# Two transformer blocks in float32r halves: four weight units side by side behind a sandwich norm, a reordered preamble, wide stick-breaking blocks first, and the last square of a row norm summed by TensorE

## The chip, the cores and the metric

The kernel runs as one program on one core of a Trainium2 chip. The metric is the time of one execution in microseconds (us) on the device, as the median of the runs; lower is better.

## The reference

Two blocks of two layers each work on x, 512 tokens by 1024 channels, in float32. Cut to what matters here:

```python
# first block, for each of two layers
h = rms_norm(x, attn_pre_g[l]); proj = h @ w_in[l]            # 1024 x 3080: q, k, v of 4 difference heads and
                                                              # 8 forgetting heads, and 8 forget logits
oa = rms_norm(diff_attention(rotary(qa), rotary(ka), va, lam), diff_sub_g[l]) * (1 - lam_init)
ob = forgetting_attention(qb, kb, vb, log_sigmoid(f_logit + forget_bias[l]))
x = x + rms_norm(concat(oa, ob) @ w_out[l], attn_post_g[l])   # sandwich norm: before and behind
h = rms_norm(x, ffn_pre_g[l])
y = (silu(h @ w_gate[l]) * (h @ w_up[l])) @ w_down[l]         # 2816 wide
x = x + rms_norm(y, ffn_post_g[l])
# second block: stick-breaking attention (layer 0), HGRN2 (layer 1), each with a squared-relu MLP (4096)
q, k, v = split(rmsnorm(x, g) @ w_qkv)                        # 16 heads of 64; q and k normed per head
z = q @ k.T * scale                                           # per block of 128 queries, causal
log_between = reverse_cumsum(log_sigmoid(-z)) - log_sigmoid(-z)
weights = exp(log_sigmoid(z) + log_between)                   # strictly causal
x = x + (weights @ v) @ w_o
```

## The kernel before

Everything is kept transposed: `xT` holds x as 8 tiles of 128 channels by 512 tokens. Each weight matrix is used in units, one unit being 128 output channels. A unit's weights (128 x 1024, 512 KB) are loaded by a DMA on SP's queue into `w_raw[:, slot]` (slot 0 or 1, in turn), rounded by GpSimd to float32r as `w_hi` (L571) and subtracted by VectorE to the rest `w_lo` (`split_low`, L1181). The activations are likewise halves, `h_hi` from ScalarE (L1679) and `h_lo` from VectorE (`low_part`, L1111), and TensorE runs for each of 8 input tiles hi x hi, hi x lo and lo x hi (`products`, L618): 24 products of 128 x 512 for a unit, into the PSUM bank `acc[slot]`.

The order on every engine is written out by hand and kept by counting semaphores; each engine works strictly in its own program's order. A load of a slot waits until the unit before it in that slot was split (`w_split`), a rounding waits until that unit's products ended (`unit_done`), a unit's products wait for its split and for the bank to be taken (`evacuated`).

The places that matter:

- The preamble. SP loads x; TensorE transposes it tile by tile when all of it has landed (L691), VectorE copies it to `xT` (L1096). ScalarE's queue loads gains and small constants. The first two units are rounded and split by GpSimd (`split`, L557 and L559). VectorE computes the angles of the rotary tables behind the first norm, ScalarE sine and cosine.
- A norm ahead of products (`pre_norm`, with `low_part` and `add_pair`). The row scale `rstd` is applied when a unit is taken, so products can run before it is known. `side_by_side` runs units 0 and 1 as each `h_lo` tile comes, the second `LAG` = 3 tiles behind, and sums squares by a product with ones (`sum_pair`, L631); ScalarE then forms `rstd` (L1687, L1689).
- A sandwich norm. Behind the output and the down products the squares of the 8 tiles are added up one after the other on VectorE (`add_square`, L1106), summed over channels by TensorE (`sum_squares`, L682), and `update_x` scales y (L1300), adds it to `xT` (L1308) and forms `h_lo` of the next norm, tile by tile.
- Attention of a layer: 8 pairs of heads, p = 0 to 7, each in 12 slots k. TensorE's slots hold the scores, transposes and weighted sums of pair p, and between them the three units (q, k, v) of pair p+1. Step p = -1 is the start: units 0 to 2, and the forget product (`wf`) into `sc[0]`. `take_qk` (L1220) frees the bank of q or k, `rotate` makes q and k from it.
- Stick-breaking (`sb_pair`): 8 pairs, 12 slots each, four blocks of 128 queries in turn; block t has (t+1) x 128 keys for two heads: scores (L874) into `z_pair[t % 2]`, ScalarE's three passes (L1834, L1836, L1838), VectorE's `log_weights` (L1375 to L1384), transposes (L904), exponential (L1870), weighted sum (L916). A block's transposes come two steps of three slots behind its scores, its weighted sum in the same step. `vraw` is taken by VectorE (L1402) at slot 0 and transposed by TensorE (L891) at slot 2. Behind the last pair there are six more slots (`TAIL`) shared with the first output units.

## Time and profile before

| | us |
|---|---|
| median of 3 runs | 2741.28 |
| lowest, highest | 2739.74, 2741.86 |
| the profiled execution | 2739.28 |
| its span in the profile | 2737.6 |
| TensorE products busy | 2617.0 (96%) |
| VectorE, ScalarE, GpSimd busy | 1653.0, 745.1, 459.5 |
| granted TensorE clock, mean | 0.982 |

The span is from the first to the last instruction of the profiled execution. Products overlap, so a busy TensorE need not be at its best pace: a product shows some 0.39 us, but they start 0.227 us apart.

### The profile page before, as it was taken

The numbers are of one execution on the slowest core, as the hardware profiler recorded it, in microseconds if no ns is written. First come the engines' busy times: TensorE is split into PE (matmuls) and PEld (weight loads), VectorE is DVE, ScalarE is ACT, GpSimd is POOL, SyncE is SP. The second block draws the span as 40 slices with busy tenths as digits, with TensorE's granted clock in tenths as the row PEclk, the third lists the DMA queues.
The fourth block names the chain that finished last, engine by engine and source line by source line (L and its number), as shares of the span: only waits on it lengthen the run. The fifth ranks groups of instructions, "written<-read, shape, count | busy, mean of one in ns | idle before, by whom it ended". The sixth has DMA issues, their size and how long they took to land.

```text
span 2737.6 us, 38434 instructions
## 1 busy us (share of the span) xinstructions
PE 2617.0 (96%) x12249; PEld 2058.1 (75%) x12249; DVE 1653.0 (60%) x2625; ACT 745.1 (27%) x1386; POOL 459.5 (17%) x458
## 2 busy tenths in 40 slices
PE   6999899999799989999989989999999999999999
PEld 4676688888567668888856657888888887788887
DVE  6765566454675566646467775644558888564452
ACT  2333232120233323212045552100024555210000
POOL 4111121112111111111211101111111110111111
PEclk8999999999899999999999999999999999999999
DMA  3221233332222123333311112333332211233333
GB/s 93 62 58 51 62 100 96 96 100 85 63 55 62 48 72 96 99 96 96 92 54 54 54 39 85 94 98 97 95 99 63 62 54 54 70 99 93 100 97 96
DMA packets 417268, 214.76 MB, mean 78 GB/s; under 512 B 6820, under 2 KB 416015, under 8 KB 417167
## 3 DMA queue, kind: packets, MB, share of 16 engines
q1 hardware_dynamic: 416144, 212.89, 26.9%
q8 instruction: 57, 0.93, 0.1%
q10 hardware_dynamic: 1022, 0.58, 0.1%
q14 instruction: 45, 0.36, 0.0%
HBM read 211.34 MB, written 2.10 MB: 78 GB/s over the span
## 4 chain that ended last, share of the span: by engine, by line
PE 82%; DVE 8%; ACT 4%; issue 4%; DVEq 0%; DMA 0%; POOL 0%; SPq 0%; ACTq 0%; POOLq 0%
PE acc L618 72%; PE sc L720 2%; PE sc L1016 2%; DVE xT L1308 1%; PE tp L739 1%; PE po L762 1%; ACT h_hi L1679 1%; ACT scratch L1836 1%; DVE scratch L1381 1%; PE tp L874 1%; ACT scratch L1834 1%; DVE w_lo L1181 0%; PE po L1039 0%; DVE scratch L1248 0%; DVE scratch L1375 0%
## 5 line engine op out<-in xcount | busy, mean ns | idle before, releaser
L618 PE MATMUL acc<-h_hi,w_hi 128*128 128x512 f32 x2048 | 846.3, 413 | 49.5 <-DVE h_lo L1111 30.6
L618 PE MATMUL acc<-h_hi,w_lo 128*128 128x512 f32 x2048 | 805.1, 393 | 0.0
L618 PE MATMUL acc<-h_lo,w_hi 128*128 128x512 f32 x2048 | 803.8, 392 | 0.0
L571 POOL TENSOR_SCALAR w_hi<-w_raw 128x1024 fp32r<-128x1024 f32 x398 | 422.4, 1061 | 2255.7 <-PE acc L618 2255.7
L1181 DVE TENSOR_TENSOR w_lo<-w_raw,w_hi 128x1024 fp32r<-128x1024 f32 x398 | 484.9, 1219 | 70.2 <-POOL w_hi L571 69.7
L618 PEld LDWEIGHTS acc<-h_hi,w_hi 128*128 128x128 f32 x2048 | 387.7, 189 | 182.7 <-DVE h_lo L1111 48.3
L618 PEld LDWEIGHTS acc<-h_hi,w_lo 128*128 128x128 f32 x2048 | 387.4, 189 | 84.4
L618 PE MATMUL acc<-mid_hi,w_hi 128*128 128x512 f32 x1120 | 441.9, 395 | 6.6 <-DVE mid_lo L1639 3.2
L618 PEld LDWEIGHTS acc<-h_lo,w_hi 128*128 128x128 f32 x2048 | 388.8, 190 | 78.2 <-issue 6.7
L618 PE MATMUL acc<-mid_lo,w_hi 128*128 128x512 f32 x1120 | 440.4, 393 | 0.0
L618 PE MATMUL acc<-mid_hi,w_lo 128*128 128x512 f32 x1120 | 439.5, 392 | 0.0
L618 PEld LDWEIGHTS acc<-mid_hi,w_hi 128*128 128x128 f32 x1120 | 211.8, 189 | 55.1 <-DVE w_lo L1181 3.9
L618 PEld LDWEIGHTS acc<-mid_lo,w_hi 128*128 128x128 f32 x1120 | 211.8, 189 | 45.5 <-issue 2.9
L618 PEld LDWEIGHTS acc<-mid_hi,w_lo 128*128 128x128 f32 x1120 | 211.8, 189 | 44.3 <-issue 0.8
L1451 DVE TENSOR_TENSOR xT<-xT,acc 128x512 f32 (+1 forms) x80 | 55.0, 687 | 203.1 <-PE acc L618 203.1
L1897 ACT ACTIVATE mid_hi<-scratch 128x512 f32 x64 | 40.5, 633 | 471.9 <-DVE scratch L1490 471.9
L1487 DVE TENSOR_TENSOR scratch<-acc,rstd 128x512 f32<-128x512 f32 x64 | 44.2, 691 | 130.7 <-PE acc L618 122.1
L1248 DVE CUSTOM_DVE_ANT_0 scratch<-sc,mask_row 128x128 f32<-128x128 f32 (+3 forms) x128 | 62.3, 487 | 85.5 <-PE sc L720 46.0
L1747 ACT ACTIVATE scratch<-scratch,stat 128x128 f32<-128x128 f32 (+3 forms) x128 | 72.1, 563 | 133.8 <-DVE stat L1248 133.8
L1805 ACT ACTIVATE mid_hi<-scratch 128x512 f32 x44 | 27.8, 632 | 213.0 <-DVE scratch L1347 213.0
L1341 DVE TENSOR_TENSOR scratch<-acc,rstd 128x512 f32<-128x512 f32 x44 | 30.4, 691 | 84.2 <-PE acc L618 84.2
L1682 ACT ACTIVATE scratch<-yT 128x512 f32 x32 | 20.2, 632 | 208.8 <-DVE yT L1317 137.4
(288 smaller groups left out, 2513.3 us busy)
## 6 DMA issues: line engine op xcount, KB each, us to landing
w_raw<-in_mlp_w_dram SPq DMA_DIRECT2D x128, 512.0 KB, 4.0
w_raw<-in_w_in_dram SPq DMA_DIRECT2D x48, 512.0 KB, 3.8
w_raw<-in_w_gate_dram SPq DMA_DIRECT2D x44, 512.0 KB, 3.7
w_raw<-in_w_up_dram SPq DMA_DIRECT2D x44, 512.0 KB, 3.7
w_raw<-in_w_down_dram SPq DMA_DIRECT2D x32, 512.0 KB, 4.0
w_raw<-in_hg_w_in_dram SPq DMA_DIRECT2D x32, 512.0 KB, 4.0
w_raw<-in_sb_w_qkv_dram SPq DMA_DIRECT2D x24, 512.0 KB, 3.7
w_raw<-in_w_out_dram SPq DMA_DIRECT2D x16, 512.0 KB, 4.0
```

The costliest lines, as they stand in the source:

```text
L571: nc.gpsimd.tensor_scalar(w_hi[:, slot], w_raw[:, slot], 1.0, 1.0, ALU.mult, ALU.mult).then_inc(w_rounded, 1)
L618: mm = pe.matmul(bank[:], w[:, k], r[:, k], start=(k == 0 and i == 0), stop=(k == k_tiles - 1 and i == 2))
L720: mm = pe.matmul(sc[m][:, 0:n], qT[p % 2][r, t * P:t * P + P], kT[p % 2][r, 0:n], start=True, stop=(p < NDIFF))
L1016: mm = pe.matmul(sc[lv % 2][:, b * HD:b * HD + HD], x[:, b * P:b * P + P], right, start=True, stop=True)
L1181: TT(w_lo[:, slot], w_raw[:, slot], w_hi[:, slot].bitcast(F32), ALU.subtract).then_inc(w_split, 1)
L1248: v.tensor_tensor_reduce(prob[k % 4][:, 0:n], sc[k % 2][:, 0:n], mask_row[:, S - n:S], 1.0, BIG, ALU.add, ALU.min, stat[:, k % 4:k % 4 + 1 ...
L1341: TT(up, acc[1][:], rstd[:], ALU.mult).then_inc(evacuated[1], 1)
L1451: TT(dst, dst, acc[slot][:], ALU.add).then_inc(evacuated[slot], 1)
L1487: TT(gate, acc[i][:], rstd[:], ALU.mult).then_inc(evacuated[i], 1)
L1747: ACTV(prob[k % 4][:, 0:n], prob[k % 4][:, 0:n], ACT.Exp, bias=stat[:, k % 4:k % 4 + 1], scale=-1.0, accum_out=stat[:, 4 + k % 4:5 + k % 4 ...
L1805: ACTV(mid_hi[:, c % 2, ds(j, 1)], hid, ACT.Copy).then_inc(mid_hi_ready, 1)
L1897: ACTV(mid_hi[:, c % 2, ds(2 * m + i, 1)], hid, ACT.Copy).then_inc(mid_hi_ready, 1)
```

## The change

It does four things.

1. Behind the sandwich norms (and in the preamble) `side_by_side` runs four units instead of two, with lags 0, 1, 4 and 5 tiles; at the start of stick-breaking it runs three, and the fourth behind them. The two more units have room for their halves in free parts of `mid_hi` and `mid_lo` (`ex_hi`, `ex_lo`) and products in free banks (`po`, and `tp[1]` or `sc[1]`). GpSimd rounds them with `round_extra`, VectorE splits them with `split_extra`: in `update_x` one ahead of the wait for `rstd` and one at tile 3. The first pair behind then has two units between its slots instead of three. The forget product goes to `tp[0]`, its low half is formed by VectorE.
2. The preamble: x is transposed quarter by quarter of the tokens as it lands, copied half by VectorE and half by ScalarE; constants move from ScalarE's queue to SP's, ahead of the weights; the wait in front of the first weight load goes; VectorE splits the first units; one step of the cosine moves to ScalarE.
3. Stick-breaking takes its blocks in the order 512, 384, 256, 128 keys; the transposes of v move from slot 2 to slot 4.
4. Of a sandwich norm's and a second-block norm's eight squares the last isn't added by VectorE: TensorE sums it by a second product with ones into the same bank.

```diff
-LAG = 3
+LAGS = [0, 1, 4, 5]
-        sb_soft = [two_heads(t, (4096, 4864)[t % 2]) for t in range(NB)]
+        sb_soft = [two_heads(NB - 1 - t, (4864, 4096)[t % 2]) for t in range(NB)]
...
@@ block.sync
+            for i, w in enumerate((lam_q1, lam_k1, lam_q2, lam_k2)):
+                sp.dma_start(lam_in[:, i], w.partition_broadcast(P)).then_inc(consts_in, 16)
+            sp.dma_start(pos_i, positions.rearrange("b s -> (b s)").partition_broadcast(P)).then_inc(consts_in, 16)
+            sp.wait_ge(vec_consts, 1)
+                for c in (0, 8, HD, HD + 8):
+                    sp.dma_start(lconst[c:c + 8, :, 2], forget_bias.rearrange("l h -> h l")).then_inc(consts_in, 16)
...
@@ block.gpsimd
+            pool.sem_inc(w_split, 2)
+            def round_extra(half):
+                for slot in range(2):
+                    round_unit(half, slot, ex_hi[:, slot], None)
-            split(0, 0, 8)
-            split(0, 1, 8)
+            for slot in range(2):
+                round_unit(0, slot, w_hi[:, slot], None)
+            round_extra(1)
...
-                steps(nc.gpsimd.tensor_scalar(wf_hi, wf_raw[:], 1.0, 1.0, ALU.mult, ALU.mult))
-                steps.wait()
-                nc.gpsimd.tensor_tensor(wf_lo, wf_raw[:], wf_hi.bitcast(F32), ALU.subtract).then_inc(wf_split, 1)
+                nc.gpsimd.tensor_scalar(wf_hi, wf_raw[:], 1.0, 1.0, ALU.mult, ALU.mult).then_inc(wf_rounded, 1)
-                round_units(half + 1, U_GU0 // 2)
-                round_units(half + 1 + U_GU0 // 2, (U_LAYER - U_GU0) // 2)
+                round_units(half + 2, U_GU0 // 2 - 1)
+                round_extra(half + U_GU0 // 2 + 1)
+                for slot in range(2):
+                    round_unit(half + U_GU0 // 2 + 2, slot, w_hi[:, slot], 2 * half + U_GU0 + slot + 3)
+                round_units(half + U_GU0 // 2 + 3, (U_LAYER - U_GU0) // 2 - 2)
+                round_extra(half + U_LAYER // 2 + 1)
...
@@ block.tensor
+            def side_by_side(half, base, n, banks):
+                units = [unit(half, i, h_hi, h_lo, ready=h_ready, base=base, fresh=True) for i in range(2)]
+                units += [extra_unit(half + 1, i, bank, base) for i, bank in enumerate(banks)]
+                for k in range(KD + LAGS[len(units) - 1]):
+                    if k in (2, 4, 6, KD):
                         sum_pair(n * (KD // 2), (k - 1) // 2)
+                    for ops, lag in zip(units, LAGS):
+                        if 0 <= k - lag < KD:
+                            run(ops[3 * (k - lag):3 * (k - lag) + 3])
+            def sum_squares(added, n, a):
+                pe.wait_ge(square_added, added + KD - 1)
                 pe.wait_ge(aux_free, a)
+                pe.matmul(aux[:], ones[:, 0:P], square_sum, start=True, stop=False)
+                pe.wait_ge(square_ready, n + KD)
+                pe.matmul(aux[:], ones[:, 0:P], square[(KD - 1) % 2], start=False, stop=True).then_inc(aux_done, 1)
+            for t in range(NB):
+                pe.wait_ge(x_in[t], 16)
+                if t >= 2:
+                    pe.wait_ge(x_left, t - 1)
+                    pe.wait_ge(x_right, t - 1)
+                for j in range(KD):
+                    mm = pe.transpose(x_banks[t % 2][j // NB][:, j % NB * P:j % NB * P + P], x_tok[:, t, j * P:j * P + P],
+                                      ident[:])
...
+                        side_by_side(half0, l * 16, 2 * l, (po, tp[1]))
+                        work = products(tp[0], h_hi, h_lo, wf_hi, wf_lo, 8, wf_done,
+                                        lambda k: pe.wait_ge(wf_split, l + 2) if k == 0 else None)
+                    elif p + 1 < PAIRS:
+                        for u in range(max(3 * (p + 1), 4), 3 * (p + 1) + 3):
+                            work += unit(half0 + u // 2, u % 2, h_hi, h_lo, behind=1 if u < 6 else 0)
-                        for slot, name, i in ((6, "rot_q", 0), (9, "rot_k", 1)):
+                        for slot, name, i in ((6 if p >= 0 else 0, "rot_q", 0), (9 if p >= 0 else 6, "rot_k", 1)):
...
-                            side_by_side(half, l * 16 + 8, 2 * l + 1)
-                            with pe.Fori(1, n) as j:
+                            side_by_side(half, l * 16 + 8, 2 * l + 1, (po, sc[1]))
+                            gate_up(half + 2, 1)
+                            with pe.Fori(3, n) as j:
...
@@ sb_pair
+                    if not current:
+                        side_by_side(U_SB // 2, block2_norm(0)[0], 2 * LAYERS, (tp[1],))
+                        work = extra_unit(U_SB // 2 + 1, 1, po, block2_norm(0)[0])
-                    step, n = 4 * p + t, (t + 1) * P
+                    step, b = 4 * p + t, NB - 1 - t
+                    n = (b + 1) * P
-                    if current and k == 2:
+                    if current and k == 4:
                         pe.wait_ge(aux_free, aux_n)
...
@@ block.vector
+            split_low(0, 0)
             for j in range(KD):
                 low_part(0, j, gains[:, G_ATT_PRE + j:G_ATT_PRE + j + 1])
+                if j == 0:
+                    split_low(0, 1)
                 if j % 2:
                     add_pair(0, 0, j)
+                if j in (5, 7):
+                    split_extra(1, (j - 5) // 2)
...
+                v.wait_ge(wf_rounded, l + 1)
+                TT(wf_lo, wf_raw[:], wf_hi.bitcast(F32), ALU.subtract).then_inc(wf_split, 1)
...
+                def update_x(g, x_n, scaled, n, norm, half):
+                    split_extra(half, 0)
                     v.wait_ge(rstd_ready, l * 4 + g + 2)
                     for j in range(KD + 1):
+                        if j == 3:
+                            split_extra(half, 1)
...
+                        if c == 0:
+                            gate_up(0, acc, 2)
+                            gate_up(1, (po, sc[1]), 0)
+                        with v.Fori(2 if c == 0 else 0, n) as j:
+                            gate_up(j, acc, 1)
```

## Rows read from the trace of the kernel before

**Rows 1.** A piece of the chain that ended last, with its products.
```profile
342.83 348.76 PE acc L618 x1536
```

**Rows 2.** TensorE's waits: line, what it waited for, us in total, times, longest.
```profile
PE acc L618 <- DVE h_lo L1111: 30.6, 23, 6.5
PE acc L618 <- DVE yT L1220: 13.8, 2, 10.5
PE aux L891 <- DVE yT L1402: 7.5, 7, 2.9
```

**Rows 3.** Stretches: us, busy PE, PEld, DVE, ACT, POOL (instructions), clock, DMA share, GB/s.
```profile
0.00:65.50 65.50, 40.08 (x143) 28.43 (x143) 40.38 (x74) 16.66 (x25) 34.00 (x57) 0.87 0.33 97
65.50:92.90 27.40, 26.09 (x128) 19.04 (x128) 21.17 (x50) 9.15 (x24) 2.63 (x3) 1.00 0.23 58
312.50:342.80 30.30, 20.35 (x59) 11.63 (x58) 23.04 (x33) 14.29 (x23) 2.09 (x2) 0.83 0.12 35
691.40:742.40 51.00, 35.23 (x111) 22.47 (x110) 32.27 (x46) 13.21 (x21) 10.39 (x10) 0.83 0.17 46
1368.60:1435.80 67.20, 53.83 (x213) 34.78 (x212) 43.88 (x61) 31.69 (x49) 8.26 (x7) 0.92 0.19 55
1435.80:1612.10 176.30, 168.03 (x932) 115.56 (x931) 135.72 (x181) 97.40 (x144) 18.81 (x18) 1.00 0.19 54
1612.10:1647.80 35.70, 24.15 (x145) 15.94 (x145) 23.33 (x31) 14.19 (x20) 0.00 (x0) 0.86 0.05 15
```

**Rows 4.** The preamble: two pieces of the chain that ended last, one of the timeline.
```profile
2.20 6.41 DMA yT<-in_x_dram
17.16 4.18 DVE h_lo L1111 x2
49.13 0.76 PE L618 MATMUL acc<-h_hi,w_hi 128*128 128x512 f32 x1 [10.51 <-DVE yT L1220]
```

**Rows 5.** VectorE's groups by shape, six steady stick-breaking pairs.
```profile
L1181 DVE TENSOR_TENSOR w_lo<-w_raw,w_hi 128x1024 fp32r<-128x1024 f32 x18 | 21.9, 1218 | 3.0 <-POOL w_hi L571 3.0
L1381 DVE TENSOR_TENSOR_SCAN scratch<-sb_restart,scratch 128x512 f32<-128x512 f32 x12 | 14.0, 1212 | 0.2
...
L1384 DVE TENSOR_TENSOR scratch<-tp,scratch 128x1024 f32<-128x1024 f32 x6 | 7.3, 1225 | 0.2
```

**Rows 6.** Timeline of TensorE where the second block's first sum stands.
```profile
1692.50 1.02 PE L682 MATMUL aux<-scratch,ones 128*128 128x512 f32 x2
```

**Rows 7.** Timeline of VectorE at the end of pair 0, layer 0.
```profile
92.04 0.69 DVE L1229 TENSOR_TENSOR scratch<-yT 128x512 f32<-128x512 f32 x1
```

**Rows 8.** DMA issues near 316: line, count, KB each, us to landing.
```profile
w_raw<-in_w_up_dram SPq DMA_DIRECT2D x1, 512.0 KB, 3.7
```

**Rows 9.** Timeline: GpSimd and VectorE at the same time (start, us, instruction).
```profile
38.45 0.43 DVE L1151 TENSOR_SCALAR scratch<-scratch 128x512 f32<-128x512 f32 x1
38.82 1.04 POOL L571 TENSOR_SCALAR w_hi<-w_raw 128x1024 fp32r<-128x1024 f32 x1 [1.14 <-PE acc L618]
38.91 1.23 DVE L1153 TENSOR_SCALAR scratch<-scratch 128x512 f32<-128x512 f32 x1
...
696.82 2.83 POOL L596 TENSOR_TENSOR mid_hi<-wf_raw,mid_hi 128x1024 fp32r<-128x1024 f32 x1
697.48 2.71 DVE L1308 TENSOR_TENSOR xT<-xT,yT 128x512 f32<-128x512 f32 x1
```

**Rows 10.** Timeline of the norm ahead of the gate products, layer 0.
```profile
317.74 0.75 DVE L1300 SCALAR_TENSOR_TENSOR yT<-yT,layer_gain,rstd 128x512 f32<-128x512 f32 x1 [1.47 <-ACT rstd L1689]
...
320.01 0.75 DVE L1111 SCALAR_TENSOR_TENSOR h_lo<-xT,layer_gain,h_hi 128x512 fp32r<-128x512 f32 x1
...
329.78 0.75 DVE L1111 SCALAR_TENSOR_TENSOR h_lo<-xT,layer_gain,h_hi 128x512 fp32r<-128x512 f32 x1
```

**Rows 11.** Timeline of TensorE behind the last stick-breaking pair.
```profile
1642.33 0.33 PE L904 MATMUL tp<-ident,scratch 128*128 128x128 f32 x1 [2.30 <-DVE scratch L1384]
```

**Rows 12.** ScalarE's groups by shape, the same six pairs.
```profile
L1838 ACT ACTIVATE scratch<-scratch 128x1024 f32<-128x1024 f32 x6 | 6.4, 1062 | 0.2
```

More of the change, by code:

```diff
@@ L121, in added_base @@
 def added_base(n):
-    return 2 + KD * n
+    return 2 + (KD - 1) * n
 def block2_norm(i):
@@ L632, in sum_pair, with unit @@
                           stop=last).then_inc(aux_done if last else square_summed, 1)
-            def unit(half, slot, hi, lo, k_tiles=8, ready=None, base=0, fresh=False, squares=None):
+            def unit(half, slot, hi, lo, k_tiles=8, ready=None, base=0, fresh=False, behind=0):
                 def before(k):
@@ L828, in _, with gate_up @@
                         run(unit(half0 + U_OUT // 2 + m, i, mid_hi[:, 0], mid_lo[:, 0]))
-                sum_squares(added_base(2 * l), A + AUX["norm_att_post"])
-                def gate_up(half):
-                    run(unit(half, 0, h_hi, h_lo))
-                    run(unit(half, 1, h_hi, h_lo))
+                sum_squares(added_base(2 * l), l * 32 + 8, A + AUX["norm_att_post"])
+                def gate_up(half, behind=0):
+                    run(unit(half, 0, h_hi, h_lo, behind=behind))
+                    run(unit(half, 1, h_hi, h_lo, behind=behind))
                 for kind, c, u in FFN_ORDER:
@@ L1334, in _ @@
                             take(half + j, 0)
-                            TT(gate, acc[0][:], rstd[:], ALU.mult).then_inc(evacuated[0], 1)
-                            split_low(half + j + 1, 0)
+                            TT(gate, banks[0][:], rstd[:], ALU.mult).then_inc(evacuated[0], 1)
+                            if splits:
+                                split_low(half + j + splits, 0)
                             v.wait_ge(gate_log, g + 1)
@@ L1390, in take_raw @@
                     take(half + u // 2, u % 2)
-                    TT(raw, acc[u % 2][:], rstd[:], ALU.mult).then_inc(evacuated[u % 2], 1)
+                    bank = po if u == 3 and not previous else acc[u % 2]
+                    TT(raw, bank[:], rstd[:], ALU.mult).then_inc(evacuated[u % 2], 1)
                 def normed(i):
```

257 lines of the change are left out of this document (132 added, 125 removed).

## The prediction

> **What bounds the kernel now.** I read the page's busy shares only to see that TensorE hardly rests, then the waits of TensorE, which say where it does, then a table of stretches, and then the order of time inside each stretch. The pace is 1536 products in 348.76 us [rows 1]: 0.227 us each, 5.45 us for a unit of 24. Nothing in the change removes a product, so a gain can only come from time in which TensorE runs none or runs at the lower of its two levels. The longest waits are for `h_lo` of a new norm (30.6 us), for the first `take_qk` of a layer (13.8 us in two) and for `vraw` in stick-breaking (7.5 us in seven) [rows 2]. The stretches show them at work: 20.35 us busy of 30.30 where a norm is followed by the gate products, granted clock 0.83; 35.23 of 51.00 between the layers, also 0.83; 40.08 of 65.50 before pair 0; 24.15 of 35.70 at the end of stick-breaking [rows 3]. In the long middle, 168.03 of 176.30, there is little to win.
>
> **The preamble.** Before, all of x lands after 2.20 + 6.41 = 8.6 us, then come 32 transposes and eight copies by VectorE; the first `h_lo` starts at 17.16 and takes 4.18 us for two, beside GpSimd's two-input splits; after the two units TensorE waits 10.51 us, until 49.13, for `take_qk` [rows 4]. The change transposes each quarter of x as it lands, shares the copies with ScalarE and loads the weights earlier, but behind nine small loads on SP's queue. I place x at 11.7, and the first weights at 13.5; rounding 1.04 and splitting 1.22 [rows 5] puts `h_lo` 0 near 16 and the first product near 16.7, `h_lo` 4 near 22.8. TensorE, slow at first, has four units (96 products, 21.8 us) and four sums to run; from step 4 on the stage is 75 products and three sums of 0.92 us [rows 6], 19.8 us, begun at about 25.8: end 45.7. VectorE's chain for sines (29.4 to 42.1, held by the exponential behind the row norm) ends in time for its two `take_qk`. Then the forget product (5.5 us) and two rotations (0.92 each) with 0.4 us of wait: pair 0 starts at 53.5 with its successor's first unit done.
>
> **Pair 0 loses its cover.** Its cover falls from 72 to 48 products, 5.45 us. But VectorE ends its rotation of key 1 at 92.04 + 0.69 just when the scores of pair 1 start, and is busy 21.17 of 27.40 us [rows 3, 7]: pair 0 is not TensorE's. Unit 4 is now wanted at once, while its low part is formed behind `raw_f` and `vraw`, 2.4 us into the pair. Going through the slots, VectorE's pauses shorten by 1.2 us only: 26.2 us. Pair 1 starts at 79.7, before at 92.9: **-13.2**. Bounds -18 (the whole 5.45 gained) and -8 (loads 5 us late).
>
> **Between the layers.** The reordered last square takes VectorE's add (0.7) and its handoff out of the chain: 0.85 us. The extra unit's first split goes ahead of `rstd`'s use, and its load was only issued when a buffer came free: 3.7 us to land [rows 8], 1.04, 1.22; update_x starts 0.9 late. GpSimd's two-input split of `wf` goes, beside which L1308 took 2.71 us for about 0.69 [rows 9]: -2.0. The second extra split lies inside update_x: +1.2. So `h_lo` 4 moves by only +0.1, to 711.6 when ready, and the four units end 18.9 us later, at 730.5; the last sum stands behind twelve more products, but `rstd` is still in time. The forget product, two rotations and 0.4 us of wait follow: pair 0 at 738.25, before 742.4. With 26.2 for pair 0 pair 1 starts at 764.45, before at 769.7: -5.3.
>
> **Rounds against splits.** GpSimd's rounds now fall into update_x. A round of 1.04 us at 38.82 stands beside a VectorE instruction that started at 38.91 and took 1.23, while its twins on the same shape took 0.43 [rows 9]. So a round costs VectorE between 0 and 0.8 us; I take 0.8 at each boundary, and 1.5 here, where the rounds of `wf` come too. Between the layers: **-3.8**, bounds -8 and +1.
> The Trainium skill (SBUF — State Buffer, Who interferes with whom) says that VectorE with two SBUF inputs and a reading GpSimd instruction exclude each other for a whole instruction. The rows agree; by the rule alone two rounds of 1.04 could cost 2.1 us at each of four boundaries where I took 0.8: some 5 us longer, which is a part of the second rival below.
>
> **Before the gate products, twice.** update_x began at 317.74 and `h_lo` 0 at 320.01, `h_lo` 4 at 329.78 [rows 10]. New: update_x 0.3 earlier (the square saves 0.85, the split waiting for its load takes it back), `h_lo` 4 0.9 later, so it is ready at 331.43; the 75 products and the two sums still to come, 18.9 us, and 0.1 of wait end at 350.45. The four gate and up tiles pile up on VectorE: the third gate is taken at 361, and the split of the unit behind it comes 1.2 us late. Before, the dense run began at 342.83; now it begins at 351.65 with two units (10.9 us) more done, 2.1 less; minus 0.8 for rounds, two places: **-2.6**, bounds -8 and +3.
>
> **Into stick-breaking.** Here three units go side by side and the fourth behind. TensorE has nine products a step where it had three, so the last sum is later: I place `rstd` at 1400.5, some 3 us after its old time. Then the chain square, head sum, logarithm, exponential for q and again for k has only one unit as cover, and unit 4's split follows it before the first scores: 1416. Pair 0 has 48 products and the wide block first, so VectorE's chain sets it: 23 us. Pair 1's scores come at 1439, before 1435.8: +3.2, with the rounds **+4.0**; bounds -3 (cover holds) and +9.
>
> **Wide blocks first.** In six steady pairs the narrow block is now last, so `vraw` isn't queued behind the longest chain; its transposes also move two slots on. That frees 7.5 - 2.9 = 4.6 us [rows 2]: **-4.6**, bounds -8 and +4. The step with the wide block in bank pair 0 now also waits for the wide exponential, as the other did: nothing. At the end, before, the transposes of the widest block started at 1642.33 after 2.30 us of wait [rows 11] and the stretch lasted 35.70 [rows 3]. The wide chain is three ScalarE passes of 1.06 and on VectorE 1.2 + 0.4 + 2 x 1.21 + 1.23, 5.3 us [rows 5, 12]: with it first, I get scores of the third block at 12, its logarithms at 14.2, VectorE done with both last blocks at 19.8, output at 23.5; some of it at the lower clock: 25.5. **-10.2**, bounds -13 and -5.
>
> **The summed square.** In three norms TensorE did not wait for the sum, so the second ones-product is pure work: the one there is two passes of 1.02 us together, some 0.1 of it beside its neighbours [rows 6], so 0.9 each: **+2.7**, bounds 0 and +3.
>
> **Sum.** -13.2 - 3.8 - 2.6 + 4.0 - 4.6 - 10.2 + 2.7 = -27.7 against the profiled execution's 2739.3 (span 2737.6): 2711.6. The median of the runs is 2.0 above it: **2713.6 us**.
>
> **Rivals.** First, the cover holds: pair 0 of both layers gains the whole 5.45 (8.5 more), stick-breaking starts without the tail of its norm chain (6 more), and rounds block nothing (3.1). For it speaks that TensorE was busy 26.09 us of 27.40 in pair 0; against it that VectorE ended there just in time. 2713.6 - 17.6 = 2696.
> Second, VectorE becomes the bound: pair 0 isn't shorter (2.4), the steady pairs gain nothing (4.6), the tail only 7 (3.2), rounds cost twice (4): 2728. For it speaks VectorE's 135.72 of 176.30 us busy with its chains in order [rows 3].
> Third, slower: the wide block ahead of the others. From its scores to its transposes lie six slots, half of a pair of 29.4, some 12.5 us; the chain is 3.2 + 5.3, the scores 1, and up to 1.9 of `vraw` and split before it: 11.5. If ScalarE's order (a high part that waits for VectorE's copy) stretches it beyond 12.5, each of eight pairs pays the excess. It turns the forecast to slower by more than 0.2% from 4.2 us per pair, a chain of 16.7; at 4.7 it gives 2751. Against it: ScalarE was busy only 97.40 of 176.30.
> Fourth, the change doesn't do what it says: blocks reordered give nothing (14.8) and the weights behind the small loads land 7.5 us late: 2736.
>
> **How the numbers follow.** Forecast 0.58, first rival 0.17, second 0.15, third 0.04, fourth 0.06. Within 0.2% (5.5 us) is about what a measurement of this kernel can tell from no change. So faster 0.90, same 0.06, slower 0.04. The bounds of the terms, not all on one side, span about 13 us to either side, and reach the first two rivals: 2695 to 2729; the third and fourth are left out.
>
> **What the profile would show.** Pair 0's first scores near 53.5 with a 10.51 us wait gone, and VectorE nearly without pause in pair 0; at 312.5 a dense TensorE from the fifth `h_lo` on and `rstd` 4 to 5 us later than before; no VectorE instruction of 2.7 us at the layer's start; TensorE waiting for `normed` before the first stick-breaking scores, none for `vraw` later; a last pair of some 25 us. It would be wrong if update_x stretched with each round, if the third gate were later, or if transposes of a wide block were waited for in every pair.

## The result and the profile after

| | before | after |
|---|---|---|
| median of the runs beside each other (14 of each), us | 2740.22 | 2747.16 |
| lowest, highest | 2737.31, 2741.86 | 2741.27, 2754.34 |
| the profiled execution | 2739.28 | 2743.68 |
| its span | 2737.6 | 2741.9 |
| TensorE products busy | 2617.0 | 2623.3 |

The ratio of the times is 1.0027, with a 95% interval of 1.0020 to 1.0034: slower, by 6.9 us, and the lower end of the interval lies at the 0.2% that the prediction named as its bound. "Before" and "after" are the two kernels from here on. The forecast was 2713.6, 33.6 us away and outside its range of 2695 to 2729. The third rival, slower through ScalarE's order in stick-breaking, had been given 0.04.

The first view of after is the table of stretches, at the same places of the work as [rows 3] (us, then busy time of PE, PEld, DVE, ACT and POOL with instructions, granted clock, DMA share, GB/s). The fourth row is one more: pairs 0 and 1 of layer 1.

```profile
0.00:55.10 55.10, 42.97 (x167) 32.51 (x167) 32.59 (x70) 19.58 (x30) 28.34 (x55) 0.91 0.38 116
55.10:86.20 31.10, 23.72 (x103) 15.98 (x102) 21.88 (x51) 9.04 (x24) 3.03 (x2) 0.89 0.19 51
682.60:730.60 48.00, 39.22 (x137) 26.22 (x136) 31.29 (x44) 13.22 (x21) 9.67 (x10) 0.89 0.18 49
730.60:789.10 58.50, 50.86 (x232) 35.61 (x231) 42.03 (x98) 19.31 (x50) 5.15 (x4) 0.94 0.20 55
1358.10:1434.40 76.30, 58.83 (x238) 37.61 (x237) 46.91 (x62) 32.38 (x49) 8.17 (x7) 0.91 0.17 49
1434.40:1622.10 187.70, 170.93 (x934) 117.25 (x933) 141.01 (x181) 97.53 (x144) 24.68 (x18) 0.98 0.17 51
1622.10:1648.70 26.60, 18.29 (x123) 11.48 (x123) 19.63 (x29) 13.34 (x20) 0.00 (x0) 1.00 0.07 21
```

Against [rows 3] the losses and gains are on two sides. Up to pair 0 it is 55.10 for 65.50, and the last pair with its tail takes 26.60 where it took 35.70: this is what the change was forecast to do. But pair 0 lasts 31.10 for 27.40, with TensorE busy 23.72 of it and a clock of 0.89, and the six steady pairs of stick-breaking last 187.70 for 176.30 with TensorE busy only 2.9 us more in them: it now stands still where it hardly did.

The waits of TensorE (line, what it waited for; us in total, times, longest) name both places.

```profile
PE acc L633 <- DVE h_lo L1146: 33.9, 16, 6.9
PE tp L903 <- ACT yT L1942: 18.5, 8, 2.8
PE acc L633 <- DVE w_lo L1168: 14.0, 10, 3.6
```

The wait for `h_lo` is 3.3 us longer than in [rows 2]. The waits for `take_qk` (13.8 us) and for `vraw` (7.5 us) of [rows 2] are gone. What has grown are two kinds that were small before, as the same view of the kernel before shows:

```profile
PE tp L874 <- ACT yT L1870: 6.4, 9, 2.3
...
PE acc L618 <- DVE w_lo L1181: 1.0, 2, 0.5
```

The wait for the exponential of stick-breaking went from 6.4 to 18.5 us, that for a weight's low half from 1.0 to 14.0: 25.1 more, against 21.3 removed. Smaller ones changed too: the wait for the sum of squares behind the sandwich norms fell from 10.1 to 2.8 us, and that for the rotated keys rose from 1.3 to 5.3.

### The profile page after: what moved, and what is told of

It reads as the page before. It is cut to its first block, busy times and chain, and to the rows that moved or that the text cites. A ratio compares the mean times of both kernels' runs of the same rounds, so it can differ in the third digit from the quotient of the medians.

```text
span 2741.9 us, 38338 instructions
## 1 busy us (share of the span) xinstructions
PE 2623.3 (96%) x12263; PEld 2063.1 (75%) x12263; DVE 1647.9 (60%) x2617; ACT 747.8 (27%) x1391; POOL 460.8 (17%) x454
## 4 chain that ended last, share of the span: by engine, by line
PE 80%; DVE 10%; issue 4%; ACT 4%; DMA 1%; POOL 0%; DVEq 0%; SPq 0%; ACTq 0%; POOLq 0%
PE acc L633 68%; PE sc L1048 2%; PE sc L740 2%; DVE w_lo L1168 1%; DVE scratch L1447 1%; PE tp L633 1%; PE tp L763 1%; PE po L786 1%; PE po L633 1%; DVE scratch L1441 1%; ACT scratch L1908 0%; ACT scratch L1906 0%; DVE xT L1356 0%; DVE scratch L1293 0%; DMA w_raw<-in_w_in_dram 0%
## 5 line engine op out<-in xcount | busy, mean ns | idle before, releaser
L633 PE MATMUL acc<-h_hi,w_hi 128*128 128x512 f32 x1968 | 815.4, 414 | 45.9 <-DVE h_lo L1146 33.9
L633 PE MATMUL acc<-h_hi,w_lo 128*128 128x512 f32 x1968 | 776.1, 394 | 0.0
L633 PE MATMUL acc<-h_lo,w_hi 128*128 128x512 f32 x1968 | 774.7, 394 | 0.0
L1168 DVE TENSOR_TENSOR w_lo<-w_raw,w_hi 128x1024 fp32r<-128x1024 f32 x390 | 475.5, 1219 | 69.0 <-POOL w_hi L576 69.0
L633 PEld LDWEIGHTS acc<-h_hi,w_hi 128*128 128x128 f32 x1968 | 373.7, 190 | 169.0 <-DVE h_lo L1146 43.5
L633 PEld LDWEIGHTS acc<-h_hi,w_lo 128*128 128x128 f32 x1968 | 373.1, 190 | 82.3 <-issue 1.5
L633 PEld LDWEIGHTS acc<-h_lo,w_hi 128*128 128x128 f32 x1968 | 374.3, 190 | 79.8 <-issue 11.3
L1877 ACT ACTIVATE mid_hi<-scratch 128x512 f32 x44 | 27.8, 632 | 203.5 <-DVE scratch L1402 203.5
```

The costliest lines, as they stand in the source:

```text
L633: mm = pe.matmul(bank[:], w[:, k], r[:, k], start=(k == 0 and i == 0), stop=(k == k_tiles - 1 and i == 2))
L1168: TT(w_lo[:, slot], w_raw[:, slot], w_hi[:, slot].bitcast(F32), ALU.subtract).then_inc(w_split, 1)
L1877: ACTV(mid_hi[:, c % 2, ds(j, 1)], hid, ACT.Copy).then_inc(mid_hi_ready, 1)
```

## Where the 33 us went, read from the traces

Times at which the same piece of work starts, after minus before, give the account of the two profiled executions. It covers 32.1 of the 33.6 us; the other 1.5 are there because the median of after lies 3.5 us above its profiled execution, where 2.0 was added in the forecast. Each part is rounded by itself.

| part | predicted | measured |
|---|---|---|
| preamble and pair 0 of layer 0 | -13.2 | -6.6 |
| between the layers, to the end of pair 1 | -3.8 | +1.0 |
| two gate boundaries, with the pairs up to them | -2.6 | -4.8 |
| into stick-breaking, its pair 0 with it | +4.0 | +9.0 |
| six steady pairs | -4.6 | +11.4 |
| last pair and tail, to the second block's first sum | -10.2 | -9.4 |
| from there to the end, with the summed square of three norms | +2.7 | +3.9 |
| sum | -27.7 | +4.4 |

**Pair 0.** The timeline of after (start, us, engine, instruction, in brackets the idle time before it and what ended it), cut to what matters:

```profile
55.10 0.49 PE L740 MATMUL sc<-scratch 64*128 64x128 f32 x4
55.21 0.69 DVE L1335 TENSOR_TENSOR yT<-tp,rstd 128x512 f32<-128x512 f32 x1 [0.28 <-PE tp L633]
...
57.15 1.22 DVE L1168 TENSOR_TENSOR w_lo<-w_raw,w_hi 128x1024 fp32r<-128x1024 f32 x1
...
58.42 0.80 PE L633 MATMUL acc<-h_hi,w_hi 128*128 128x512 f32 x1 [2.83 <-DVE w_lo L1168]
...
59.01 0.63 PE L633 MATMUL acc<-h_lo,w_hi 128*128 128x512 f32 x1
...
64.39 0.42 DVE L1293 CUSTOM_DVE_ANT_0 scratch<-sc,mask_row 128x256 f32<-128x256 f32 x1 [5.82 <-PE sc L740]
```

TensorE has done unit 3 and has only unit 4, whose low half VectorE forms behind `raw_f`, `vraw` and the first maximum of pair 0: it stands still for 2.83 us. Then the products show 0.63 us and start 0.43 apart, where [rows 1] has 0.227. The eight of them that come before the second scores take twice their time, and VectorE waits 5.82 us for these scores, with nearly all of pair 0 still ahead of it. How long the pair lasts differs between executions: in the four experiments that leave its code alone (the first, third, fourth and sixth) it took 28.5 to 30.0 us in layer 0, and pair 1 behind it 28.7 where after has 27.2; both pairs together took 57.2 to 58.8, in after 58.3, before 54.5.

**A steady pair of stick-breaking.** ScalarE's part of the pair that started at 1496.0, and VectorE's copy that it waits for:

```profile
1508.14 1.03 ACT L1942 ACTIVATE yT<-sc 128x1024 f32<-128x1024 f32 x1 [0.24 <-PE sc L933]
1513.24 0.64 ACT L1946 ACTIVATE mid_hi<-yT 128x512 f32 x1 [4.08 <-DVE yT L1492]
1513.78 0.58 ACT L1906 ACTIVATE scratch<-sc 128x512 f32<-128x512 f32 x1
...
1516.30 0.63 ACT L1921 ACTIVATE yT<-yT 128x512 f32<-128x512 f32 x1
1518.57 0.63 ACT L1916 ACTIVATE yT<-yT 128x512 f32<-128x512 f32 x1 [1.63 <-DVE yT L1458]
1519.10 0.79 ACT L1942 ACTIVATE yT<-tp 128x768 f32<-128x768 f32 x1
```
```profile
1509.72 1.81 DVE L1447 TENSOR_TENSOR_SCAN scratch<-sb_restart,scratch 128x384 f32<-128x384 f32 x2
1511.56 0.96 DVE L1450 TENSOR_TENSOR scratch<-tp,scratch 128x768 f32<-128x768 f32 x1
1512.44 0.68 DVE L1492 COPY yT<-po 128x512 f32<-128x512 f32 x1
```
```profile
1514.89 0.87 PE L933 MATMUL tp<-ident,scratch 128*128 128x128 f32 x6
...
1519.95 0.49 PE L903 MATMUL tp<-scratch 64*128 64x128 f32 x4 [2.80 <-ACT yT L1942]
```

From 1509.2 to 1513.2 ScalarE does nothing: at its head is the high part of the last pair's output (`sb_high`, L1946), which needs VectorE's copy (L1492), and that is queued behind the chain of the second block, now 384 keys wide. Behind the high part stand the third block's three passes, the row scale of q, and the square of k, which waits 1.63 us more for VectorE. The exponential of the second block is behind all of these and starts at 1519.10, though its transposes were done at 1515.8; the fourth scores need its bank and come 2.80 us late.

**Between the layers** GpSimd and VectorE stand beside each other as forecast:

```profile
688.74 0.75 DVE L1348 SCALAR_TENSOR_TENSOR yT<-yT,layer_gain,rstd 128x512 f32<-128x512 f32 x1
...
689.73 1.39 POOL L576 TENSOR_SCALAR mid_hi<-w_raw 128x1024 fp32r<-128x1024 f32 x1 [2.16 <-DMA w_raw<-in_w_in_dram]
690.13 1.52 DVE L1348 SCALAR_TENSOR_TENSOR yT<-yT,layer_gain,rstd 128x512 f32<-128x512 f32 x1
...
693.91 1.49 POOL L607 TENSOR_SCALAR mid_hi<-wf_raw 128x1024 fp32r<-128x1024 f32 x1 [0.19 <-POOL wf_raw L604]
694.42 1.52 DVE L1154 TENSOR_TENSOR scratch<-scratch 128x512 f32<-128x512 f32 x1
```

Two VectorE instructions took 1.52 us where their kind takes 0.75 and 0.68, as the one of 1.23 in [rows 9]: 1.6 us more, where the prediction had 1.5.

## The experiments

Every time is a median, beside runs of the kernel before on the same chip: 2739.47 us for the first four, 2740.02 for the next four, 2739.30 for the last three. After was timed apart from them (before was 2740.22 there), and its runs lie 13 us apart, so a difference of medians against after is good to a few us; where it matters the difference of the profiled executions stands beside it.

| run | us (lowest to highest) | ratio to before, 95% interval |
|---|---|---|
| ScalarE's order mended | 2725.5 (2724.6 to 2727.0) | 0.9949, 0.9936 to 0.9963 |
| unit 4 split early | 2732.8 (2731.4 to 2733.9) | 0.9978, 0.9967 to 0.9988 |
| narrow block first | 2737.4 (2733.8 to 2740.7) | 0.9993, 0.9984 to 1.0002 |
| old square, second block | 2743.9 (2736.0 to 2748.1) | 1.0015, 1.0005 to 1.0025 |
| all three mended | 2708.5 (2708.0 to 2710.4) | 0.9886, 0.9871 to 0.9901 |
| high part only | 2730.7 (2726.5 to 2735.2) | 0.9968, 0.9957 to 0.9979 |
| three ahead | 2698.8 (2697.5 to 2701.3) | 0.9848, 0.9835 to 0.9862 |
| mended, narrow first | 2713.1 (2710.5 to 2713.6) | 0.9898, 0.9883 to 0.9913 |
| three ahead, extra buffer | 2699.4 (2698.7 to 2700.3) | 0.9852, 0.9835 to 0.9868 |
| two ahead | 2715.8 (2714.7 to 2716.9) | 0.9909, 0.9893 to 0.9926 |
| v at slot 2 | 2699.5 (2697.8 to 2701.0) | 0.9849, 0.9833 to 0.9865 |

**1. ScalarE's order mended.**

```diff
@@ scalar, sb_pair
                         if previous or t >= 2:
                             sb_exp(p if t >= 2 else p - 1, (t + 2) % NB)
-                        if previous and k == 6:
-                            sb_high(p - 1)
+                        if following and k == 9:
+                            raw_norm(1, k, 9, 10)
                         softplus_log(t)
+                        if previous and k == 6:
+                            sb_high(p - 1)
...
-                        raw_norm(1, k, 8, 10)
+                        raw_norm(1, k, None if current else 8, 10)
```

> The changed kernel with ScalarE's order in stick-breaking mended: the high part of the last pair's output goes behind the three passes of the third block instead of ahead of them, and the square of raw k behind the exponential of the second block. Theory (ScalarE's order is what the wide-first order pays for): the wait of TensorE for sb_exp of the last pair or block at the narrow block's transposes, 18.5 us in 8 in the changed kernel, falls under 5; the steady pairs, 30.7 to 32.5 us, come to 28.5 to 29.5; total 2747 - 6 x 2.2 = 2734, within 2728 to 2739. Rival (VectorE's wide chain is too long for its six slots, whatever ScalarE does): the wait changes its releaser to VectorE and stays above 2 us a pair, total 2744 to 2748.

Measured: 2725.5, 21.7 us below the changed kernel (16.7 in the profiled executions). In the six steady pairs the list of TensorE's waits is empty. The same stretch of ScalarE, in the pair that started at 1491.1:

```profile
1503.22 1.03 ACT L1944 ACTIVATE yT<-sc 128x1024 f32<-128x1024 f32 x1 [0.26 <-PE sc L933]
1505.29 0.60 ACT L1906 ACTIVATE scratch<-sc 128x512 f32<-128x512 f32 x1 [1.04 <-PE sc L903]
...
1508.31 0.63 ACT L1948 ACTIVATE mid_hi<-yT 128x512 f32 x1 [1.10 <-DVE yT L1492]
...
1510.89 0.81 ACT L1944 ACTIVATE yT<-tp 128x768 f32<-128x768 f32 x1 [0.71 <-PE tp L933]
1511.81 0.63 ACT L1916 ACTIVATE yT<-yT 128x512 f32<-128x512 f32 x1
```

The second block's exponential comes 7.67 us behind the first's, where it was 10.96, and waits for its own transposes alone. The stretch of that whole pair:

```profile
1491.10:1519.20 28.10, 28.10 (x158) 19.36 (x157) 23.50 (x31) 16.46 (x24) 4.20 (x3) 1.00 0.19 57
```

TensorE is busy 28.10 of 28.10 us, and each steady pair is 28.0 us long, 167.9 for six. The rival, VectorE's chain too long for its slots, falls: the chain was not touched. The gain is more than expected: in the profiled executions the six pairs went from 187.7 to 167.9 us, well under the 176.3 of before [rows 3]. Of these 19.8 us the waits were 16.7; the other 3.1 are what two of the pairs at the low clock had been longer than their neighbours.

**2. Unit 4 split early.**

```diff
@@ vector, attention
+                        if p == -1 and k == 9:
+                            split_low(half0 + 2, 0)
-                        if p >= 0 and (k == 0 or k in (4, 8) and p + 1 < PAIRS):
+                        if p >= 0 and (k == 0 and p > 0 or k in (4, 8) and p + 1 < PAIRS):
@@ vector, sb_pair
+                    if not current and k == 9:
+                        split_low(half + 2, 0)
-                    if current and (k == 0 or following and k in (4, 8)):
+                    if current and (k == 0 and previous or following and k in (4, 8)):
```

> The changed kernel with the split of unit 4 moved on VectorE from behind vraw and the first maximum of pair 0 to the step before (between the take of k and its rotation), in both layers and in stick-breaking. Theory (pair 0 lost its cover because its only next unit was not split): TensorE's 2.8 us without products in pair 0 and the low clock behind it go, VectorE no longer waits 5.8 us for the second scores; pair 0 of layer 0 lasts 26 instead of 31.1 us, of layer 1 27 instead of 29.7; total 2747 - 8 = 2739. Rival (VectorE is the bound of pair 0 whatever is split when): pair 0 gives 1 us or less in each layer, total 2745.

Measured: 2732.8, 14.3 below the changed kernel where 8 was expected. In the profiled executions it gains 4.8 us in layer 0, 4.1 in layer 1 and 4.6 from the last norm to pair 1 of stick-breaking, where after waits 3.6 us for the same unit's low half; later stretches give 3 back, so that 10.4 is left. Pairs 0 and 1 of layer 0:

```profile
54.30:79.90 25.60, 21.00 (x105) 14.28 (x104) 20.85 (x50) 8.80 (x24) 3.02 (x2) 1.00 0.20 56
79.90:108.60 28.70, 28.48 (x130) 20.41 (x130) 20.08 (x48) 10.29 (x26) 2.10 (x2) 0.94 0.21 56
```

Pair 0 takes 25.6 us (31.1), in layer 1 as well (29.7). Pair 1 now starts at 79.9, where the prediction had put it at 79.7; that is in part luck, since pair 0 starts 0.8 later and lasts 0.6 less than was forecast. The rival falls. Pair 1, though, is 28.7 where before it was 27.2: its row shows a clock of 0.94. TensorE had stood 2.63 us ahead of its first scores, waiting for VectorE's rotation, and its first six products showed 0.63 us or more:

```profile
79.85 0.71 PE L740 MATMUL sc<-scratch 64*128 64x128 f32 x4 [2.63 <-DVE scratch L1274]
```

**3. Narrow block first.** The order of the blocks undone on all engines, v's transposes back at slot 2.

```diff
-                    step, b = 4 * p + t, NB - 1 - t
+                    step, b = 4 * p + t, t
@@ vector, log_weights
-                    n = (NB - t) * P
+                    n = (t + 1) * P
@@ tensor and scalar
-                    if current and k == 4:
+                    if current and k == 2:
```

> The changed kernel with the stick-breaking order of before: blocks of 128, 256, 384, 512 keys in turn and the transposes of v at slot 2; all else as changed. Theory (the wide block first costs the steady pairs 11.6 us and gives the tail 9.5): the steady pairs return to 29.4 us and the last pair with its tail to 35.7; the first pair of stick-breaking gets its old 20 to 24 us for 27.8; total 2747 - 2 - 5 = 2740. Rival (the steady pairs are slower through the rounds, loads or clock that the four units brought): they stay near 31 us and the total is 2747 + 9 = 2756.

Measured: 2737.4, 9.7 below the changed kernel, now within 0.2% of before. The six steady pairs are back at 177.0 us (before 176.3) and from the last pair's first scores to the end of the tail it is 34.4 us, where after has 26.6 and before 35.7. Pair 0 of stick-breaking takes 23.0 us, where after has 27.8. Rounds and loads do not slow the steady pairs: the rival falls. As it stood, the wide-first order cost more (10.7 us in the steady pairs, 4.7 in pair 0) than its tail gave (7.8).

**4. Old square in the second block.**

```diff
@@ tensor, sum_squares in the second block's norms
-                pe.matmul(aux[:], ones[:, 0:P], square_sum, start=True, stop=False)
-                pe.wait_ge(square_ready, n + KD)
-                pe.matmul(aux[:], ones[:, 0:P], square[(KD - 1) % 2], start=False, stop=True).then_inc(aux_done, 1)
+                    pe.matmul(aux[:], ones[:, 0:P], square_sum, start=True, stop=True).then_inc(aux_done, 1)
@@ vector, add_tile
-                    if not final:
-                        add_square(squares, added, j, i)
+                    add_square(squares, added, j, i)
```

> The changed kernel with VectorE adding the last square again in the three norms of the second block where TensorE goes through without a pause; the sandwich norms keep the second product. Theory (a product that fills no gap is paid in full): minus one product of 1.0 to 1.3 us each, total 2747 - 3.5 = 2743.5. Rival (it lies beside its neighbours): within 0.5 us of the changed kernel.

Measured: 2743.9, 3.2 less, as the theory had it, but this alone shows nothing: the runs scatter by 12 us and the intervals of the two kernels overlap. The profiled executions show it better. In after's timeline the two products stand one behind the other, 0.86 apart:

```profile
1693.02 1.02 PE L698 MATMUL aux<-scratch,ones 128*128 128x512 f32 x2
1693.88 1.02 PE L700 MATMUL aux<-scratch,ones 128*128 128x512 f32 x2
```

From the first norm's sum to the second's it is 348.39 us before and 348.38 here, 349.25 in after; from the third's to the end 351.42 before, 351.41 here, 352.28 in after. So a product costs its 0.86, 2.6 in all. From the first sum to the end after had lost 3.9 us against before, this one 0.5; what is beyond the products lies between the second and the third sum, a stretch that lasts 344 to 349 us in the executions profiled here.

**5. All three mended.** The diffs of 1, 2 and 4 together.

> The changed kernel with the edits of the first, second and fourth experiment together: ScalarE's order in stick-breaking, the early split of unit 4, the old last square in the second block's norms. Theory (the three are separate causes at separate places): the gains add up, 21.7 + 14.3 + 3.2 = 39 below 2747.2, less some 4 where the second experiment's gain was shorter low-clock times in stick-breaking that the first removes too: 2712, within 2706 to 2716. Rival (they share a cause, the low clock above all): 2720 or more.

Measured: 2708.5, 38.7 below the changed kernel; the three single gains add up to 39.2 (in the profiled executions 35.7 against 31.9). So they are separate causes, and the overlap of 4 us that was expected did not show. This is the changed kernel with the order of work on ScalarE and VectorE altered and the second block's extra products gone. It is 5.1 us under the forecast for the change, but not all its parts are as forecast: in the profiled executions the steady pairs give 8.4 us where 4.6 was forecast, the last pair and its tail 7.5 where 10.2 was.

**6. High part only.** The move of `sb_high` from the first experiment, without that of the square.

> The changed kernel with only the first half of the first experiment's edit: the high part goes behind the three passes of the third block, the square of raw k stays ahead of the exponential of the second block. Theory (the high part, which waits for VectorE's copy behind its second chain, is what delays everything behind it): this half alone gives most of the 21.7 us, 2728. Rival (the square that waits for VectorE's take is as much to blame): only a third to a half, 2737 to 2740, steady pairs of 29.5 to 30 us.

Measured: 2730.7, 16.5 of the 21.7 us. TensorE's wait for the second block's exponential falls in the six steady pairs, first in after, then here:

```profile
PE tp L903 <- ACT yT L1942: 16.2, 6, 2.8
```
```profile
PE tp L903 <- ACT yT L1942: 5.3, 6, 1.0
```

A pair is 28.9 us, 173.6 for six: 14.1 of the 19.8 us that the first experiment gained there. So the high part is some three quarters of the cause and the square the rest.

**7. Three ahead in attention.** On the kernel of 5: unit 3 goes back between the slots of pair 0 and is rounded and split as an ordinary unit. Three more things change with it: unit 4's split in attention goes back to slot 0 of pair 0, since unit 3 now stands before it; behind a layer's last norm `update_x` no longer has a second extra split in it; and the fourth unit of stick-breaking gets an ordinary buffer.

```diff
-                        side_by_side(half0, l * 16, 2 * l, (po, tp[1]))
+                        side_by_side(half0, l * 16, 2 * l, (po,))
-                        for u in range(max(3 * (p + 1), 4), 3 * (p + 1) + 3):
-                            work += unit(half0 + u // 2, u % 2, h_hi, h_lo, behind=1 if u < 6 else 0)
+                        for u in range(3 * (p + 1), 3 * (p + 1) + 3):
+                            work += unit(half0 + u // 2, u % 2, h_hi, h_lo, behind=1 if u == 4 else 0)
@@ vector, attention
+                        if p == -1 and k == 5:
+                            split_low(half0 + 1, 1)
@@ gpsimd, before the loop over the layers (and alike at its end)
-            round_extra(1)
+            round_unit(1, 0, ex_hi[:, 0], None)
```

> The kernel of the fifth experiment with three units ahead instead of four in attention (unit 3, q of pair 1, goes back between the slots of pair 0) and the fourth unit of stick-breaking from the ordinary slot; the gate stage keeps four. Theory (pair 0 with 48 products is VectorE's and too thin, so the fourth unit ahead is paid in the step before and comes back only in part): the step before pair 0 is 5.45 us shorter in layer 1 and 2 to 4 in layer 0, pair 0 lasts 27.3 for 25.6, pair 1 27.1 for 28.7: 2 x 4 faster than the fifth. Rival (the norm chain and the rotations need the fourth unit as cover): TensorE waits for take_qk or the rotation instead, equal or slower than the fifth.

Measured: 2698.8, 9.7 below the fifth (6.7 in the profiled executions: 2.5 in layer 0 and 6.0 in layer 1, less 2 into stick-breaking). Pairs 0 and 1 of layer 0, and the stretch between the layers:

```profile
51.00:78.30 27.30, 26.03 (x127) 18.99 (x126) 21.79 (x51) 9.04 (x24) 2.57 (x3) 1.00 0.21 59
78.30:105.50 27.20, 26.95 (x128) 19.30 (x128) 20.07 (x48) 10.24 (x26) 2.92 (x3) 1.00 0.21 59
675.10:716.80 41.70, 33.54 (x113) 22.64 (x111) 30.37 (x44) 13.21 (x21) 8.23 (x9) 0.84 0.21 56
```

The stretch between the layers is 41.7 us, in the fifth it was 47.9; pair 0 takes 27.3 and fills TensorE to 26.03, so it costs 1.7 more than with 48 products, and pair 1 takes 27.2 in both layers, where in the fifth it took 27.2 and 28.8. The fourth unit side by side made the stage in front 4.3 us longer in layer 0 and 6.2 in layer 1 (in the latter one split of 1.2 us in `update_x` went with it), for a pair 0 that could not use the room: VectorE is busy for some 21 us of it in any case. The rival falls.

**8. Mended, narrow first.** The fifth kernel with the order of the third.

> The kernel of the fifth experiment with the narrow block first and v's transposes at slot 2. Theory (wide first is worth its tail of 9.5 us and, once ScalarE's order is mended, 1.3 us in each steady pair): 10 to 17 us slower than the fifth. Rival (the mended order gives the narrow order the same pairs of 28.1 us): 8 us slower at most, the steady pairs under 28.5 us.

Measured: 2713.1, 4.6 us slower than the fifth. Neither expectation holds as written: the total is in the rival's range, but the steady pairs take 28.7 us, above its 28.5. Their stretches, first of the fifth kernel, then of this one:

```profile
1419.70:1587.60 167.90, 167.35 (x934) 115.27 (x933) 140.80 (x181) 98.66 (x144) 25.09 (x18) 1.00 0.19 57
```
```profile
1416.40:1588.50 172.10, 167.46 (x932) 115.49 (x931) 136.59 (x179) 97.40 (x144) 18.89 (x18) 1.00 0.19 56
```

Half of what the narrow order lost in each pair, against 28.0 with the wide block first, was ScalarE's order too: 29.4 came down to 28.7. Wide first gives 4.2 us over six pairs and 3.7 at the end, and loses 3.6 in pair 0 of stick-breaking, where it begins with the longest chain.

**9. Three ahead, extra buffer.** The seventh with stick-breaking's unit 3 in `ex_hi[:, 1]` and `po` again.

```diff
@@ gpsimd, behind the loop over the layers
-            round_unit(U2 // 2 + 1, 1, w_hi[:, 1], U2 + 4)
+            round_unit(U2 // 2 + 1, 1, ex_hi[:, 1], None)
```

> The kernel of the seventh experiment with stick-breaking's fourth unit again from its own buffer, rounded without a wait; attention keeps three ahead. Theory (the seventh lost some 2 us between the last norm and pair 1 of stick-breaking because its unit 3 waited for unit 1's buffer and then for its split): that stretch returns from 72.5 to 70.6 us, total 2698.8 - 2 = 2697. Rival (the stretch hangs on VectorE and the norm of q and k, not on the unit): within 0.5 us of the seventh.

Measured: 2699.4 against 2698.8: the rival's figure. In the profiled executions the stretch did go from 72.5 to 69.7 us, but with a clock of 0.93 instead of 0.86, and the runs do not show the gain; v at slot 2 below has the same buffers and a stretch of 71.5. It is not settled how much of that is the buffer and how much is where the low clock fell.

**10. Two ahead.** On the ninth.

```diff
-                        side_by_side(half0, l * 16, 2 * l, (po,))
+                        side_by_side(half0, l * 16, 2 * l, ())
+                        work = products(po, h_hi, h_lo, w_hi[:, 0], w_lo[:, 0], KD, unit_done,
+                                        lambda k: pe.wait_ge(w_split, 2 * half0 + 5) if k == 0 else None)
```

> The kernel of the ninth experiment with two units ahead in attention; unit 2 runs behind them from the ordinary buffer into the free bank, so it waits for its rounding and split, but for no row scale. Stick-breaking's two extra splits come late, so the stretch into it is not to be read. Theory (what a unit side by side gives is that it fills the pauses between the tiles of h_lo): pair 0 starts 3 to 6 us later in both layers than with three. Rival (only the free bank counts, since it ends the wait for the row scale): within 1 us.

Measured: pair 0 of layer 0 starts at 58.3 (51.8 in the ninth), and from the last sum before layer 1 to its pair 0 it is 45.0 us (40.8). So the third unit side by side is worth 6.5 and 4.2 us where the fourth cost time; the rest of the 16.4 us between the two medians lies mostly in the stretch into stick-breaking, which was not to be read. The rival falls: the free bank alone does not do it. That the pauses between the tiles are the reason is not shown, though. Unit 2 also waits here for its rounding and its split in the ordinary buffer, 3.9 us in layer 0 and 2.4 in layer 1, more than half of what was lost (TensorE's waits in the whole execution):

```profile
PE po L635 <- DVE w_lo L1173: 6.3, 2, 3.9
```

**11. v at slot 2.** The ninth with `k == 2` for `k == 4` at v's transposes, on TensorE and ScalarE.

> The kernel of the ninth experiment with the transposes of v in stick-breaking at slot 2 again. Theory (with the wide block first the narrow chain is all that vraw stands behind, so it's ready in time at slot 2 as well): within 1 us. Rival (the move to slot 4 is what spares the wait of 2.9 us): 1 to 2.9 us in each of seven pairs, 7 to 20 slower.

Measured: 2699.5 against 2699.4. The move of v's transposes is worth nothing once the narrow block is last.

## Why the prediction was wrong, step by step

- **Pace and what bounds the kernel**: right. The gains are at the places named, and the wait of 10.51 us for `take_qk` is gone.
- **The preamble**: pair 0 started at 55.1, forecast 53.5. The first product came at 19.4 instead of 16.7, because the first `h_lo` took 1.52 us and came at 17.84. The first weights were there later too, rounded at 15.62, and the `h_lo` stood behind their split. The mechanism held.
- **Pair 0 loses its cover**: the first failed step. The prediction saw that unit 4's split lies behind `raw_f` and `vraw`, 2.4 us into the pair, and still took 26.2 us from a walk through the slots. It left out that TensorE, with nothing else to do, then stands still (2.83 us), that its clock falls behind that, and that VectorE loses the time too, since its next input are the second scores. 31.1 was measured; with the split moved 25.6. The sign that was named, VectorE nearly without pause in pair 0, did not come: it was busy 21.88 of 31.10 us. For the same reason layer 1 missed: its stage in front gained 3.0 us (4.15 was forecast, 2.65 with the rounds), and pairs 0 and 1 then lost 4.0, where 1.1 was to be won.
- **Rounds against splits**: right, 1.6 us against 1.5. The two rows of 1.52 us agree with the Trainium skill's rule of a lock for the whole instruction (SBUF — State Buffer, Who interferes with whom). In both the GpSimd instruction had started first. It was not what decided. Of the rows that the prediction read as agreeing, only the one of 2.71 us is an instruction with two inputs; the one of 1.23 us has one.
- **Before the gate products**: right in sign. The two places gave 1.8 and 2.3 us, 2.6 together was forecast.
- **Into stick-breaking**: the first scores came at 1406.6, which is 1417.0 in the time of before; 1416 was forecast. Pair 0 was sized at 23 us and took 27.8; in the fifth experiment it takes 25.1. With unit 4's split moved alone (second experiment) the whole stretch is +4.4 instead of +9.0, where +4.0 was forecast: the miss is that of pair 0 in attention once more. Its parts fit less well: the first scores then come 3.2 us sooner, and pair 0 still takes 26.4. The wide block first is a cost here too, 4.7 us of pair 0 in the third experiment and 3.6 in the eighth.
- **Wide blocks first**: the second failed step, 16.0 us of the 32. The gain was read from `vraw`'s wait, which did go; the move of v's transposes had no part in that (eleventh experiment). The sentence "the step with the wide block in bank pair 0 now also waits for the wide exponential, as the other did: nothing" puts at nothing what ScalarE's queue makes of it, and the 6.4 us that TensorE waited for that very exponential before entered no term. Measured were 16.2 us of waits in the six pairs and two stretches at the low clock behind them. The third rival had the mechanism word for word, a high part that waits for VectorE's copy, but asked only whether the wide block's own chain would be late. What came late was the second block: with the order turned round, the copy stands behind a chain of 384 keys instead of 256 and the second block's exponential behind everything that waits for the copy. So the sign that was named, transposes of a wide block waited for in every pair, did not come either; the wait stood before the narrow block's scores. The price was 1.9 us a pair against before, not 4.7; it made the kernel slower only together with pair 0. "Against it: ScalarE was busy only 97.40 of 176.30" was the wrong evidence: ScalarE was busy 97.53 of 187.70 us in after, and still each pair waited for it.
- **The tail**: right, -9.4 against -10.2.
- **The summed square**: right, 0.86 for each norm against 0.9. The stretch lost 3.9 us instead of 2.7, but what is beyond 2.6 is not the products' (fourth experiment).
- **The sum**: 2713.6 was forecast, and 2708.5 is what the change gives with two queues in another order and the old square in the second block. That the two lie so close is helped by misses that cancel (fifth experiment).

## What to carry to other kernels

When work is reordered on one engine, walk the queue of every other engine once with the new order: for each instruction ask what it waits for and what stands behind it. The busy share does not show that; the longest idle time in the timeline of an engine that is far from full does. Work that runs ahead is not worth the same for each unit more: in attention the third unit was worth 6.5 and 4.2 us at its two places; the fourth cost 2.5 and 6.0, as the seventh experiment's traces have it against the fifth's, and left the stage behind it without cover.

## What had not been expected of the hardware

The lower of the two levels of TensorE's clock (1.2 GHz, shown as 0.50) stood behind some of the waits of 2.6 to 2.8 us and not behind others. In after two of the six steady pairs had it behind the same wait of 2.7 to 2.8 us, four had not. A stretch with the wait in it, and the one behind it (us, busy times, clock):

```profile
1545.00:1552.60 7.60, 4.86 (x38) 3.74 (x37) 5.19 (x8) 5.19 (x10) 0.00 (x0) 1.00 0.07 19
1552.60:1556.00 3.40, 3.40 (x8) 1.97 (x7) 1.03 (x2) 1.18 (x3) 0.00 (x0) 0.50 0.37 112
```

These two pairs lasted 32.6 and 32.4 us, the other four 30.2 to 30.9. What tells the two kinds apart is not shown. The low clock also fits the scatter of the runs: the changed kernel's times lie 13 us apart and go with the mean granted clock (0.984 at 2741.3, 0.977 at 2754.3), those of the kernel with ScalarE's order mended 2.4 us apart. That the pauses are the whole cause of the scatter was not shown: with unit 4 split early the waits in stick-breaking are still there, and its runs lie 2.5 us apart.
